# Inverse of the recurrent stage: 64-wide halves of one group against 32-wide blocks of both groups at once

## What is computed

```python
def frame_step(S, inp):
    r_t, w_t, k_t, v_t, kk_t, a_t = inp
    sa = jnp.einsum('bhvk,bhk->bhv', S, -kk_t)
    S = (S * w_t[:, :, None, :]
         + sa[..., None] * (kk_t * a_t)[:, :, None, :]
         + v_t[..., None] * k_t[:, :, None, :])
    o_t = jnp.einsum('bhvk,bhk->bhv', S, r_t)
    return S, o_t
...
u = lax.conv_general_dilated(
    u, conv_w[:, None, :], window_strides=(1,), padding=((CONV_WIDTH - 1, 0),),
    dimension_numbers=('NWC', 'WIO', 'NWC'), feature_group_count=D_CONV) + conv_b
```

## Time and profile before

| | |
|---|---|
| three runs, us | 2074.55, 2078.25, 2078.83 (median 2078.25) |
| the profiled execution, us | 2076.3 |
| its span, us | 2074.5 |
| PE busy | 1989.1 us, 96% of the span |
| DVE, POOL, ACT busy | 48%, 43%, 38% |
| recurrent stage with its inverses | from 944 to 1485 us of the span |
| one tile in it, from one `iy` of level 1 to the next | 71.65 us (1233.90 to 1305.55) |

### The profile page before, as it was taken

How to read it: one execution, slowest core, us unless ns; L and a number is a source line. 1 busy time by engine, 2 the same in 40 slices (tenths; PEclk the granted TensorE clock), 3 DMA queues, 4 the chain that set the end, 5 groups by cost and what they waited for, 6 DMA issues and landing times.

```text
span 2074.5 us, 41209 instructions
## 1 busy us (share of the span) xinstructions
PE 1989.1 (96%) x17320; PEld 1576.2 (76%) x17320; DVE 994.2 (48%) x1739; ACT 785.3 (38%) x1298; POOL 893.6 (43%) x724
## 2 busy tenths in 40 slices
PE   6989999999999999998999999999999999999997
PEld 5866667877788888886777777777787888888886
DVE  6343553232731222668667767776514366322312
ACT  4456664223432232444343334333234234322322
POOL 5333465444454545555233223323243454545542
PEclk9999999999999999999999999999999999999998
DMA  8420013522433232241111111111132332232321
GB/s 332 182 82 12 12 52 112 184 101 91 153 101 101 93 101 92 92 139 48 34 50 51 50 33 50 48 38 43 48 131 77 132 102 91 93 101 94 99 97 67
DMA packets 53062, 187.21 MB, mean 90 GB/s; under 512 B 6032, under 2 KB 7184, under 8 KB 52624
## 3 DMA queue, kind: packets, MB, share of 16 engines
q1 hardware_dynamic: 49104, 174.49, 24.8%
q10 hardware_dynamic: 3776, 10.09, 1.3%
HBM read 178.27 MB, written 6.29 MB: 89 GB/s over the span
## 4 chain that ended last, share of the span: by engine, by line
PE 89%; DVE 5%; ACT 2%; issue 1%; POOL 1%; DMA 0%; DVEq 0%; SPq 0%; ACTq 0%
PE psum L911 24%; PE psum L912 22%; PE psum L913 22%; PE psum L1377 2%; PE psum L1057 2%; PE psum L1078 1%; PE psum L1063 1%; PE psum L1353 1%; POOL wlo L787 1%; DVE psum L2287 1%; PE psum L1369 1%; PE psum L1317 1%; PE psum L1096 1%; PE psum L1341 1%; PE psum L1383 1%
## 5 line engine op out<-in xcount | busy, mean ns | idle before, releaser
L787 POOL TENSOR_TENSOR wlo<-raw,whi 128x512 fp32r<-128x512 f32 x524 | 710.3, 1377 | 993.3 <-ACT whi L1525 993.3
L911 PE MATMUL psum<-ah,whi 128*128 128x512 f32 x1256 | 524.3, 417 | 4.3 <-DVE ah L1965 3.0
L912 PE MATMUL psum<-ah,whi 128*128 128x512 f32 x1256 | 497.1, 396 | 0.0
L913 PE MATMUL psum<-ah,wlo 128*128 128x512 f32 x1256 | 495.9, 395 | 0.0
L1525 ACT ACTIVATE whi<-raw 128x1024 fp32r<-128x1024 f32 x262 | 276.0, 1054 | 323.2 <-PE psum L913 317.6
L911 PEld LDWEIGHTS psum<-ah,whi 128*128 128x128 f32 x1256 | 239.5, 191 | 67.2 <-issue 10.5
L913 PEld LDWEIGHTS psum<-ah,wlo 128*128 128x128 f32 x1256 | 239.7, 191 | 52.9
L912 PEld LDWEIGHTS psum<-ah,whi 128*128 128x128 f32 x1256 | 240.1, 191 | 44.0 <-issue 2.2
L911 PE MATMUL psum<-hidden,whi 128*128 128x512 f32 x536 | 208.7, 389 | 0.0
L913 PE MATMUL psum<-hidden,wlo 128*128 128x512 f32 x536 | 208.5, 389 | 0.0
L912 PE MATMUL psum<-hidden,whi 128*128 128x512 f32 x536 | 208.5, 389 | 0.0
(11 more groups left out here) (377 smaller groups left out, 2800.1 us busy)
## 6 DMA issues: line engine op xcount, KB each, us to landing
raw<-in_w SPq DMA_DIRECT2D x300, 512.0 KB, 3.5
raw_first<-in_w SPq DMA_DIRECT2D x14, 512.0 KB, 9.3
raw_ck<-in_w SPq DMA_DIRECT2D x8, 512.0 KB, 7.3
x<-in_x SPq DMA_DIRECT2D x4, 512.0 KB, 5.5
x_kept<-x ACTq DMA_DIRECT2D x1, 2048.0 KB, 10.3
ao_kept<-ao ACTq DMA_DIRECT2D x8, 256.0 KB, 2.3
aof<-ao_kept ACTq DMA_DIRECT2D x1, 2048.0 KB, 11.9
x<-x_kept ACTq DMA_DIRECT2D x1, 2048.0 KB, 8.7
```

The lines of the kernel that those rows point to most:

```text
L787: pool.tensor_tensor(lo_weight(place(s))[:, c], raw_of(SPLITS[s])[:, c], hi_weight(place(s)).bitcast(F32)[:, c], ALU.subtract).then_inc(lo ...
L911: pe.matmul(dst, wh, h_, start=first, stop=False)
L912: pe.matmul(dst, wh, l_, start=False, stop=False)
L913: return pe.matmul(dst, wl, h_, start=False, stop=last)
```

## The change

The inverse now works on all 16 pairs of a tile at once (`NB` = 8 columns of blocks), and up to size 32 holds only the blocks on the diagonal: 128 partitions are four blocks of 32 rows. `ix` and its transpose `iy` both grow at each of four levels, so no transposing product is needed after the first: `ip` = `ml`[level] x `ix` (plus identity, on DVE), then `ix` and `iy` from `ip`, back to back. The two halves of a 64 block are joined at the end by `jt` (with the part `mc`[:, 32:64] off the diagonal) and `jy`; `yf` collects the full result, its upper half copied by POOL. `mbs` makes its first product in pieces of 32 rows; ACT copies it to `mc`, and POOL makes the masked `ml` of all four levels at once (in `iy0`). DVE masks only the second product (`mr`). A tile has 15 slots instead of 16, with taps ahead of a slot's other work and behind it, and taps at other places of the tile (three before `mkx`, up to four behind `gnm`, two in the state chain, two at the end of the slots); `kk` stands one slot later.

```diff
-            + v[2:3] + [("lg2", j)] + v[3:] + [("kkss", j), ("kkinv", j)] + g[:1] + [("mix", j, 2)] + g[1:2] + [("kkb", j)] + g[2:3] + [("bonus", j)]
+    return (k + [("lw2", j), ("la2", j)] + r[:2] + [("mix", j, 1), ("scan", j)] + r[2:] + v[:2] + [("mix", j, 0)]
+            + v[2:3] + [("kk", j), ("lg2", j)] + v[3:] + [("kkss", j), ("kkinv", j)] + g[:1] + [("mix", j, 2)] + g[1:2] + [("kkb", j)] + g[2:3] + [("bonus", j)]
...
-TAPS = (2, 2, 3, 1, 0, 1, 2, 2, 4, 0, 2, 2, 0, 2, 0, 3)
-FIRST_TAPS = (0, 0, 2, 2, 1, 0, 2, 2, 4, 0, 2, 2, 1, 2, 0, 2)
+TAPS = ((1, 0), (2, 0), (1, 0), (2, 0), (0, 0), (0, 0), (2, 0), (1, 0), (2, 0), (0, 1), (0, 0), (1, 0), (0, 2), (4, 0), (2, 0))
...
+            front, behind = taps.pop(0)
+            got = ([ahead.pop(0)] if ahead else []) + [("conv", j, front)]
             while ahead and ahead[0][0] not in ("part", "kkinv"):
                 got.append(ahead.pop(0))
-            got.append(("conv", j, taps.pop(0)))
+            got.append(("conv", j, behind))
...
-        out += [("mks", j), ("mkx", j, 0), ("mkx", j, 1), ("inv", j, 0, 0)]
-        out += [("gnm", j - 1)] + held[:1] if j else [normed.pop(0)]
-        out += [("akv", j, 0), ("akv", j, 1), ("opv", j, 0), ("inv", j, 1, 0)] + ([("gnv", j - 1)] + held[1:] if j else []) + [("opv", j, 1)]
-        out += [("conv", j, 4)] if j else []
-        for lv in range(1, LEVELS + 1):
-            out += [("ip", j, 0, lv), ("ip", j, 1, lv)]
...
+        out += [("mks", j)] + [("conv", j, 3 if j else 0)] + [("mkx", j, 0), ("mkx", j, 1), ("inv", j)]
+        out += [("gnm", j - 1), ("conv", j, 4)] + held[:1] if j else [normed.pop(0)]
+        out += [("akv", j, 0), ("akv", j, 1), ("opv", j, 0)] + ([("gnv", j - 1)] + held[1:] if j else []) + slot() + [("conv", j, 1 if j else 0), ("opv", j, 1)]
+        for lv in range(1, LEVELS):
+            out.append(("ip", j, lv))
...
-            out += slot()
-            out += [("iy", j, 0, lv), ("iy", j, 1, lv)] + slot()
+            out += slot() + (slot() if lv in (1, 3) else [])
+            out += [("ix", j, lv), ("iy", j, lv)] + slot()
             if lv == 3 and j:
                 out.append(("aoput", j - 1))
-            if lv < LEVELS:
-                out += [("inv", j, 0, lv), ("inv", j, 1, lv)] + slot()
+        out += [("yf", j), ("jt", j)] + slot() + [("jy", j)] + slot()
...
+            out += ahead + [("conv", j, 2)]
...
+            if c in (2, 6) and j + 1 < KT:
+                out += [("conv", j, 1)] + ([("iy0", j + 1)] if c == 6 else [])
...
+                elif kind == "iy0":
+                    pool.wait_ge(mc_ready, 2 * j + 2)
+                    for lv in range(1, LEVELS):
+                        pool.tensor_tensor(ml[lv - 1], mc[:, :, 0:BL], level[lv].unsqueeze(1).to_broadcast([P, NB, BL]),
+                                           ALU.mult).then_inc(ml_ready, 1)
+                elif kind == "yf":
+                    wait_emptied(pool, ("iy", j, LEVELS - 1))
+                    pool.tensor_scalar(yf[:, :, 0:BL], iy, upper_half, None, ALU.mult).then_inc(yf_ready, 1)
...
+                    for t in range(TT):
+                        for q in range(4):
+                            n = (2 - q % 2) * BL
+                            for hh in range(2):
+                                rows, b = slice(RN * hh, RN * hh + RN), bank(("mb", j, hh))
+                                mm = pe.matmul(b[BL * q:BL * q + BL, t * CH:t * CH + n], bh[rows, t * P + BL * q:t * P + BL * q + BL],
+                                               arow[rows, t, 0, BL * q:BL * q + n], start=True, stop=True)
+                    for i, (t, own) in enumerate(own_chunks):
+                        for hh in range(2):
+                            rows, b = slice(RN * hh, RN * hh + RN), bank(("mb", j, hh))
+                            mm = pe.matmul(b[own, TT * CH + t * CH:TT * CH + t * CH + CH], bh[rows, t * P + own.start:t * P + own.stop],
+                                           arow[rows, t, 1, own], start=True, stop=True)
...
+                    pe.wait_ge(iy0_done, j + 1)
+                    for n, q in own_blocks:
+                        mm = pe.matmul(b[q, n * BL:n * BL + BL], iy[q, n, :], eye[q, q], start=True, stop=True)
+                elif kind == "ip":
+                    lv = f[2]
+                    pe.wait_ge(ml_ready, (LEVELS - 1) * j + lv)
+                    wait_emptied(pe, ("ix", j, lv - 1) if lv > 1 else ("inv", j))
+                    for n, q in own_blocks:
+                        mm = pe.matmul(b[q, n * BL:n * BL + BL], ml[lv - 1][q, n, :], ix[q, n, :], start=True, stop=True)
+                elif kind == "ix":
+                    lv = f[2]
+                    wait_emptied(pe, ("ip", j, lv))
+                    if lv > 1:
+                        wait_emptied(pe, ("iy", j, lv - 1))
+                    for n, q in own_blocks:
+                        mm = pe.matmul(b[q, n * BL:n * BL + BL], iy[q, n, :], ip[q, n, :], start=True, stop=True)
+                elif kind == "iy":
+                    for n, q in own_blocks:
+                        mm = pe.matmul(b[q, n * BL:n * BL + BL], ip[q, n, :], iy[q, n, :], start=True, stop=True)
+                elif kind == "jt":
+                    wait_emptied(pe, ("ix", j, LEVELS - 1))
+                    for n, c in joined:
+                        up, down = slice(CH * c, CH * c + BL), slice(CH * c + BL, CH * c + CH)
+                        mm = pe.matmul(b[down, n * BL:n * BL + BL], mc[up, n, BL:CH], ix[up, n, :], start=True, stop=True)
+                elif kind == "jy":
+                    wait_emptied(pe, ("jt", j))
+                    wait_emptied(pe, ("iy", j, LEVELS - 1))
+                    for n, c in joined:
+                        down = slice(CH * c + BL, CH * c + CH)
+                        mm = pe.matmul(b[CH * c:CH * c + CH, n * BL:n * BL + BL], ti[down, n, :], iy[down, n, :], start=True, stop=True)
...
+                    wait_emptied(pe, ("jy", j))
+                    pe.wait_ge(yf_ready, j + 1)
...
-                    empty(f, ix[f[2]], bank(f)[:, 0:TT * CH].rearrange("p (t n) -> p t n", t=TT))
+                elif kind == "mbs":
+                    if j:
+                        wait_filled(act, ("jt", j - 1))
+                    for hh in range(2):
+                        wait_filled(act, ("mb", j, hh))
+                        act.activation(mc[:, TT * hh:TT * hh + TT, :], bank(("mb", j, hh))[:, 0:TT * CH].rearrange("p (t n) -> p t n", t=TT),
+                                       ACT.Copy).then_inc(mc_ready, 1)
+                elif kind in ("inv", "ix"):
+                    empty(f, ix, bank(f)[:, 0:NB * BL].rearrange("p (b n) -> p b n", b=NB))
...
+                    dve.wait_ge(mc_ready, 2 * j + 2)
                     if j:
-                        wait_filled(dve, ("tav", j - 1, 0))
-                    step(dve.tensor_tensor(ip[0], ma[0], level[0].unsqueeze(1).to_broadcast([P, TT, CH]), ALU.mult))
-                    dve.tensor_tensor(iy[0], ip[0], own_eye.unsqueeze(1).to_broadcast([P, TT, CH]), ALU.add).then_inc(iy0_done[0], 1)
-                elif kind in ("mbx", "mkx"):
-                    hh, name = f[2], (kind[:2], j, f[2])
+                        dve.wait_ge(yf_ready, j)
...
+                    dve.wait_ge(mc_ready, 2 * j + hh + 1)
+                    if j:
+                        dve.wait_ge(opa_done, j)
+                    emptied_by(dve.tensor_tensor(mr[hh], bank(name)[:, TT * CH:].rearrange("p (t n) -> p t n", t=TT),
+                                                 masks[:, CH:].unsqueeze(1).to_broadcast([P, TT, CH]), ALU.mult), name)
...
-                    emptied_by(dve.tensor_tensor(ip[f[2]], bank(f)[:, 0:TT * CH].rearrange("p (t n) -> p t n", t=TT),
-                                                 level[f[3]].unsqueeze(1).to_broadcast([P, TT, CH]), ALU.mult), f)
-                elif kind == "iy":
+                    emptied_by(dve.tensor_tensor(ip, bank(f)[:, 0:NB * BL].rearrange("p (b n) -> p b n", b=NB),
+                                                 own_eye.unsqueeze(1).to_broadcast([P, NB, BL]), ALU.add), f)
+                elif kind in ("iy", "jt", "jy"):
                     wait_filled(dve, f)
-                    if f[3] == 1:
-                        dve.wait_ge(iy0_done[f[2]], j + 1)
-                    else:
-                        wait_emptied(dve, ("iy", j, f[2], f[3] - 1))
-                    emptied_by(dve.tensor_tensor(iy[f[2]], bank(f)[:, 0:TT * CH].rearrange("p (t n) -> p t n", t=TT), iy[f[2]], ALU.add), f)
+                    dst = {"iy": iy, "jt": ti[:, :, 0:BL], "jy": yf[:, :, BL:CH]}[kind]
+                    emptied_by(dve.tensor_copy(dst, bank(f)[:, 0:NB * BL].rearrange("p (b n) -> p b n", b=NB)), f)
```

More of the change, by code:

```diff
@@ L209, in rwkv_order @@
         if j + 1 < KT:
-            out += ahead
-            nxt = [[("tok", j + 1, 0)], [], [("mbs", j + 1)], [("tok", j + 1, 1)], [("tok", j + 1, 2)], [("iy0", j + 1, 0), ("iy0", j + 1, 1)]]
```

(32 more changed lines are left out.)

86 lines of the change are left out of this document (32 added, 54 removed).

## The result

| | before | after |
|---|---|---|
| four runs each, us | 2074.55 to 2078.83, median 2077.11 | 2051.68 to 2058.80, median 2057.57 |
| profiled execution, us (its span) | 2076.3 (2074.5) | 2051.68 (2049.8) |
| ratio after : before | | 0.9901, interval 0.9889 to 0.9913 |

What follows compares the result with a forecast made beforehand. PE, busy nearly all the span, bounds the kernel. Per tile 3.2 - 0.3 + 0.5 + 2.82 + 1.51 - 0.8 - 0.2 - 0.1 = 6.6 us; 39.8 for six tiles, 4.3 and 1.4 for tiles 1 and 0: 45.5 off 2076.3, 2031 us (2012 to 2050).

Steps and rivals of the forecast that it cites:

- the matmuls of the inverse: PE's inverse matmuls in one of tiles 2 to 7: 13.08 us before, 9.88 after, saving 3.2 (2.4 to 3.8).
- `jy`: Joining matmuls at the inverse's end, 32 records: 0.68 us taken as the middle of 0.38 to 1.08.
- Costed at nothing: POOL's `ml` during the state chain, DVE's and ACT's fewer passes, the same 31 taps: no effect on time.
- The wait at level 1: PE's wait for DVE's mask of `ip` goes: saves 2.82 us, and 1.51 with the clock.
- Fewer breaks: Runs of six joined at three places, fewer changes between small and large matmuls: saves 0.5 us a tile.
- `mbs`: Three times the records with fewer columns each, 0.92 us before: costs 0.3 us (0 to 0.6) a tile.
- `akv` and `gnv`: PE waits there for DVE's later `mkx` masks and the group norm behind: costs 0.8 us a tile (0 to 2.8).
- `yf`: POOL's `yf`, needed at `tav`, has cover of 0.7 us: costs 0.2 us a tile (0 to 1).
- The state chain: ACT's copy `mc` now precedes `mbx`, but masks are half as large: costs 0.1 us a tile.
- Tile 0: No level-1 wait to save, longer start, POOL's `ml` ahead of the activations' low parts: gain 1.4 us (-2 to 3.4).
- The wait only moves: Rival, chance 0.17: waits at `akv` and `gnv` add up to the old 2.8 us, clock falls again; 2053 us.
- Slower: Rival, chance 0.05: small inverse matmuls issue at large ones' pace, 34 ns a record, 14 us more a tile; 2188 us.

Runs made afterwards that it cites:

- e8_row: Changed kernel with the 64 records of `iy` at level 4 of tile 3 issued 17 times in a row; 2082.22 us.
- the second execution: The changed kernel run once more, unaltered, beside the same runs of the kernel before; 2054.33 us, ratio 0.9895.
- e2: Changed kernel with later raw weight loads fetching 64 of 1024 columns, PE's instructions unaltered; 2050.39 us, ratio 0.9883.
- e1_shift: Changed kernel with the 32 matmuls of `inv` (64 records) issued twice in tile 1 alone; 2051.18 us in one run.
- e5_dve_transpose: Changed kernel without `inv` and `ix` on PE: DVE transposes the 32 x 32 blocks of `iy`, ScalarE copies `iy`; 2024.58 us, ratio 0.9748.

## Why the prediction missed

**The step that failed** is the one on the matmuls of the inverse: "`ix` with `iy` (128 records without a break) 4 x 1.28", with the sum 9.88 and "Saved: 3.2". As prices these were right: where no gap falls in, 64 records of `ip` take 0.68 us, 128 of `ix` and `iy` 1.24, `inv` 0.68; only `jy` was off, 1.05 for 0.68. What the step left out, and "Costed at nothing" with it, is that PE must also be given the instructions. At levels 2 and 4 the new order passes 204 records (64 + 128 and two runs of six) in 4.8 us, which is 3.0 us for 128. A block took 3.47 to 4.02 where nothing else held PE up (e8_row), and 4.0 to 5.5 between those gaps of the changed kernel that stand one block apart. The kernel before passed 178 records a level in 7.2 us, 5.2 for 128, and never showed it. The price: 17.0 us in tiles 1 to 7, 2.4 a tile (14.1 in the second execution), and about 1.2 of lower clock behind the longest gap (the run of six with `lg2` took 3.65 us at 1246.10, 2.44 in the next tile).

**The other steps.** The wait at level 1 went, with its lower clock: right. Fewer breaks: right where it can be read, two runs together take 2.96 us instead of 3.2. `mbs` 1.27 us, 0.35 more: right. `akv` and `gnv` wait 1.9 us in all, not 5.6; `yf` is in time. The state chain was mis-sized: 0.95 a tile for 0.1 beside 0.3 that was there, the hop over ScalarE ahead of `mbx`. Tile 0 gained 3.4 for 1.4, in spite of POOL's 2.4.

**The sum.** The profiled gain is 20.9 us under the forecast. Gaps 17.0, clock 1.2, state chain 3.9 and `jy` 2.6 (seven tiles each) make 24.7; against that stand 3.7 at `akv` and `gnv`, 1.4 at `tav` and 2.0 in tile 0. That is 17.6; 3.3 us, some 0.5 a tile, I can't place.

**The rivals.** "The wait only moves" had the nearest time, 2053 us, by a mechanism that did not occur: there is 0.3 us a tile at `akv` and `gnv`. "Slower" asked the right question, what a record costs beyond its columns, but of the array and not of the stream. Its floor of about 25 ns from the Trainium skill (TensorE: Matmul & The Clock Gate, section "Wait — 56ns, not 53.3ns?") did not show for these tiles: in e8 128 records pass in 1.27 us, 9.9 ns apiece. The page that bears on the case is another one, on which I drew nothing: the Trainium skill (Runtime: NRT & Kernel Launch, section "Instruction fetch mechanics") says that each engine's instructions come in blocks of 256 over a DMA queue of its own, the next fetched while the current one runs, and that this is mostly hidden because issue is slower than the fill. The blocks and the queue are what the trace shows; the hiding ends here, at 3.47 us a block.

**What stays open.** Why packets come later in the changed kernel than in e8_row: ahead of the gaps of 2.44 and 2.54 us they start 3.0 and 3.1 us after the block before, where e8_row has 1.1, and with the small loads of e2 still 2.0 and 2.5. What PE waits for in the 1.3 to 1.6 us from the end of a packet to the first matmul of its block is not shown either. How long the stream can be dense before the first gap was not measured. The gap of 2.8 us ahead of `mbs` in tile 0, in all kernels, is not one of the supply; its cause was not looked into.

## What to carry to other kernels

Small matmuls that share the array are cheap in time and dear in instructions: beside the price of a group, count its records and ask how many microseconds any 128 of them, with what stands around them, take. Between gaps one block apart PE stood still here for 1.0 to 2.5 us behind blocks that it worked through in 3.0 us and for 0.2 to 0.6 behind blocks of 4.3; in the levels of the kernel before, at 5.2, it did not; the places move from tile to tile, and no semaphore explains them. Runs of large matmuls between the groups help only if the whole neighbourhood gets thinner, and records that another engine can take over (here transposes on DVE) save twice. And a copy by a second engine put ahead of a chain costs its hop even where both engines are half idle: let the engine of the chain read first.

## What was not expected of the hardware

- PE's stream of instructions: one block of 128 records in 3.47 us, at times 3.75 or 4.02 (e8_row); gaps up to 2.97 us (e1_shift) in matmuls that wait for nothing.
- DVE's transpose of the 32 x 32 blocks of a bank is no dearer than a copy out of it: 0.45 us for 128 x 256, against 0.42.
- "issue" in the list of waits can be a wait for data all the same (`akv` in e5_dve_transpose). What tells them apart is the place, since the supply's gaps wander from tile to tile with the count of records and a wait for data keeps its instruction, and the queue: in every run the gaps of the supply end 1.1 to 1.7 us after the end of one of its packets.
